# Two residual tiles turned by VectorE and two transfers instead of by TensorE, and one key weight split earlier

## The reference

```python
h = rmsnorm(x, norm_mix_w)
proj = h @ w_in                       # gated linear attention heads and differential attention heads
mixed = concatenate([o_gla, o_diff])  # both head groups, normed and gated
x = x + mixed @ w_out                 # the residual stream after the mixing branch
hc = rmsnorm(x, norm_cross_w)
q = hc @ w_cq                         # 4 heads of 256
k, v = split(rmsnorm(mem, norm_mem_w) @ w_ckv)
x = x + (softmax(q @ k.T / 16) @ v) @ w_co
return rmsnorm(x, final_norm_w)
```

## Time and profile before

| | |
|---|---|
| time, median of 3 runs | 816.72 us (815.28 to 817.65) |
| profiled execution, its own time | 814.48 us |
| its span, first to last instruction | 812.7 us |
| TensorE busy | 799.4 us, 98% |
| VectorE busy | 593.1 us, 73% |
| ScalarE busy | 422.1 us, 52% |
| mean granted TensorE clock | 0.998 of full |

### The profile page before, as it was taken

How to read it: one execution, slowest core, us unless ns; L and a number is a source line. 1 busy time by engine, 2 the same in 40 slices (tenths; PEclk the granted TensorE clock), 3 DMA queues, 4 the chain that set the end, 5 groups by cost and what they waited for, 6 DMA issues and landing times.

```text
span 812.7 us, 13040 instructions
## 1 busy us (share of the span) xinstructions
PE 799.4 (98%) x4376; PEld 669.9 (82%) x4376; DVE 593.1 (73%) x1386; ACT 422.1 (52%) x1025; POOL 98.8 (12%) x138
## 2 busy tenths in 40 slices
PE   8999999999999999999999999999999999999996
PEld 7887888888788888888888798888888888888885
DVE  6688677675678678767868877798847563367997
ACT  7766445444455345445535556543645553366453
POOL 3100111121011010111212211010010000001201
PEclk9999999999999999999999999999999999999999
DMA  8331236568365334545667368954457312107945
GB/s 283 128 84 40 85 98 170 97 111 156 66 111 112 87 95 114 108 81 98 126 132 162 108 173 269 317 125 124 146 134 177 102 66 74 57 14 153 215 86 207
DMA packets 126538, 103.41 MB, mean 127 GB/s; under 512 B 58628, under 2 KB 96648, under 8 KB 126472
## 3 DMA queue, kind: packets, MB, share of 16 engines
q1 hardware_dynamic: 98184, 66.40, 28.2%
q0 software_dynamic: 15392, 29.36, 20.1%
q10 hardware_dynamic: 12896, 6.82, 2.9%
HBM read 85.77 MB, written 33.55 MB: 147 GB/s over the span
## 4 chain that ended last, share of the span: by engine, by line
PE 83%; DVE 9%; ACT 4%; issue 2%; DMA 1%; POOL 0%; ACTq 0%; DVEq 0%
PE bank L1936 14%; PE bank L1938 14%; PE bank L1937 14%; PE banks2to L1936 9%; PE banks2to L1938 9%; PE banks2to L1937 9%; PE banks2to L2193 3%; PE banks6to L1999 3%; PE bank L2216 2%; DVE w_lo L1442 2%; DVE neg_max L1738 1%; DVE actT_lo L1441 1%; PE banks2to L2133 1%; PE bank L2218 1%; PE banks2to L2120 1%
## 5 line engine op out<-in xcount | busy, mean ns | idle before, releaser
L1938 PE MATMUL bank<-w_hi,actT_lo 128*128 128x512 f32 x412 | 161.5, 392 | 0.0
L1936 PE MATMUL bank<-w_hi,actT_hi 128*128 128x512 f32 x384 | 154.6, 403 | 0.5 <-DVE memT_lo L1441 0.2
L1937 PE MATMUL bank<-w_lo,actT_hi 128*128 128x512 f32 x384 | 149.8, 390 | 0.0
L1442 DVE SCALAR_TENSOR_TENSOR w_lo<-w_raw,vecs,w_hi 128x512 fp32r<-128x512 f32 x120 | 87.0, 748 | 24.1 <-ACT w_hi L1158 23.8
L1938 PEld LDWEIGHTS bank<-w_hi,actT_lo 128*128 128x128 f32 x412 | 77.4, 188 | 16.9
L1158 ACT ACTIVATE w_hi<-w_raw,vecs 128x512 fp32r<-128x512 f32 x120 | 83.1, 721 | 14.3 <-DMA w_raw<-in_w_ckv 8.7
L1936 PEld LDWEIGHTS bank<-w_hi,actT_hi 128*128 128x128 f32 x384 | 72.2, 188 | 16.7 <-DVE w_lo L1442 1.6
L1937 PEld LDWEIGHTS bank<-w_lo,actT_hi 128*128 128x128 f32 x384 | 72.4, 188 | 13.1
L1030 POOL TENSOR_TENSOR rs_o<-var_o,neg_half 128x1 f32<-128x1 f32 (+1 forms) x48 | 31.1, 647 | 343.8 <-DVE var_o L1766 228.5
L1938 PE MATMUL banks2to<-w_hi,actT_lo 128*128 128x512 f32 x164 | 64.0, 390 | 0.0
L1325 ACT ACTIVATE prob<-banks2to,neg_maxs 128x128 f32<-128x128 f32 (+7 forms) x64 | 46.9, 740 | 15.2 <-DVE neg_maxs L1739 15.0
(11 more groups left out here) (377 smaller groups left out, 2037.6 us busy)
## 6 DMA issues: line engine op xcount, KB each, us to landing
w_raw<-in_w_in SPq DMA_DIRECT2D x56, 256.0 KB, 3.0
out_sums<-in_w_out POOLq DMA_DIRECT2D x11, 1024.0 KB, 9.0
late_sums<-in_w_co POOLq DMA_DIRECT2D x11, 1024.0 KB, 9.2
w_raw<-in_w_ckv SPq DMA_DIRECT2D x32, 256.0 KB, 3.6
w_raw<-in_w_cq SPq DMA_DIRECT2D x32, 256.0 KB, 2.9
stage_in<-in_x SPq DMA_DIRECT2D x8, 512.0 KB, 4.6
mixT<-mixed ACTq DMA_DIRECT2D x16, 256.0 KB, 4.0
x_res<-in_x SPq DMA_DIRECT2D x8, 512.0 KB, 5.7
```

Source lines behind the costliest of these rows:

```text
L1442: return dve.scalar_tensor_tensor(dst, src, scale, hi.bitcast(F32), ALU.mult, ALU.subtract)
L1936: pe.matmul(dst, l_hi, r_hi, start=start, stop=False)
L1937: pe.matmul(dst, l_hi, r_lo, start=False, stop=False)
L1938: return pe.matmul(dst, l_lo, r_hi, start=False, stop=stop)
```

## The change

Tiles 0 and 1 of the residual take the way that tiles 4 to 7 take, with `tile_a` and `tile_b` as buffers (whole rows of 1024, so four transfers of 128 KB a tile); tiles 2 and 3 are still turned by TensorE, and their entries HT stay where they were. The entries hturn 0 and 1 stand behind xr 0 and xr 1, hback 0 and 1 at the old places of HT 0 and HT 1, and the splits HS 0 and 1 behind the HT of tiles 2 and 3. Apart from that the weight 66 is split behind K 1, ahead of the product PV 30, and no longer behind T 31.

```diff
 (stages)
             elif p == 4:
-                plan.extend([("xa", 5, t), *([("xa", 6, t)] if t < 2 else [("xr", t - 2)])])
+                plan.extend([("xa", 5, t), *([("xa", 6, t)] if t < 2 else [("xr", t - 2), ("hturn", t - 2)])])
...
-            if (p == 5 and t > 1) or (p == 6 and t < 2):
-                plan.extend([("HT", (t - 2) % 4, kk) for kk in range(2)])
+            if p == 5 and t > 1:
+                plan.extend([("hback", t - 2)])
+            if p == 6 and t < 2:
+                plan.extend([("HT", t + 2, kk) for kk in range(2)])
+                plan.extend([("HS", t, kk) for kk in range(2)])
 (with_weights)
-                where = ("Ke", 1) if k < 2 else ("T", DIFF_STEPS - 1, 1)
+                where = ("Ke", 1) if k < 3 else ("T", DIFF_STEPS - 1, 1)
 (helpers)
+        def turning_tile(t):
+            if t < 4:
+                return [(0, D, (tile_a, tile_b)[t % 2][:, :])]
+            return [(WC * j, WC, mixT[:, 6 - 2 * (t % 2) + j, 4 * P:8 * P]) for j in range(2)]
 (SyncE)
+                    for first, n, tile in turning_tile(t):
                         for band in range(P // BLK):
+                            part = tile[BLK * band:BLK * band + BLK, :]
+                            sp.dma_start(turned_rows(first, n, t, band),
...
                 elif kind == "loadw":
+                    sp.wait_ge(*turned_stored(1))
 (ScalarE)
                 elif kind == "hback":
+                    act.wait_ge(*turned_stored(t))
+                    if t < 4:
+                        act.wait_ge(*matmuls_done(("X", 4, t)))
...
                 elif kind == "HS":
+                    act.wait_ge(*residual_back(t))
 (TensorE, before a query product of the first half)
+                    if not half:
+                        pe.wait_ge(xa_dve, SPLIT_X[("HS", 1, kk)] + 1)
```

More of the change, by code:

```diff
@@ L871, in ring_job, with turned_stored, turned_no, residual_back @@
                     ps.rearrange("p (j c) -> p j c", j=4))
-        def turning_row(t):
-            return 6 - 2 * (t % 2)
-        def rest_stored():
-            return STORED * (DIFF_STEPS // 4 + 2)
+        def turning_tile(t):
+            if t < 4:
+                return [(0, D, (tile_a, tile_b)[t % 2][:, :])]
+            return [(WC * j, WC, mixT[:, 6 - 2 * (t % 2) + j, 4 * P:8 * P]) for j in range(2)]
+        def turned_stored(t):
+            first = 1 if t % 4 < 2 else 0
+            return d_mixd[t % 4], STORED * (DIFF_STEPS // 4 + (first if t < 4 else first + 2))
+        def turned_no(t):
+            return DIFF_STEPS + (t + 1 if t < 2 else t - 1)
+        def residual_back(t):
+            return d_tile[t % 4], 16 * (len(RELOADS) // 4 + (2 if t in (4, 5) else 1))
         def kept_residual(t, kk):
@@ L995, in _ @@
                     t = w[0]
-                    sp.wait_ge(md_dve, DIFF_STEPS + t - TT // 2 + 1)
-                    for j in range(2):
+                    sp.wait_ge(md_dve, turned_no(t))
+                    for first, n, tile in turning_tile(t):
                         for band in range(P // BLK):
-                            part = mixT[BLK * band:BLK * band + BLK, turning_row(t) + j, 4 * P:8 * P]
-                            sp.dma_start(turned_rows(512 * j, 512, t, band),
+                            part = tile[BLK * band:BLK * band + BLK, :]
+                            sp.dma_start(turned_rows(first, n, t, band),
                                          part.rearrange("r (b c) -> r b c", c=BLK)).then_inc(d_mixd[t % 4], 16)
@@ L1719, in _ @@
                     t = w[0]
-                    dve.wait_ge(*matmuls_done(("X", 6, 3)))
+                    if t >= 4:
+                        dve.wait_ge(*matmuls_done(("X", 6, 3)))
                     dve.wait_ge(*row_ready(t))
                     if t >= 6:
-                        dve.wait_ge(d_mixd[t % 4 - 2], rest_stored())
-                    for j in range(2):
-                        last = dve.transpose(mixT[:, turning_row(t) + j, 4 * P:8 * P], x_res[:, t, WC * j:WC * j + WC])
+                        dve.wait_ge(*turned_stored(t - 2))
+                    for first, n, tile in turning_tile(t):
+                        last = dve.transpose(tile, x_res[:, t, first:first + n])
                     last.then_inc(md_dve, 1)
@@ L1728, in _ @@
                     raw, hi, lo = kept_residual(*w)
-                    dve.wait_ge(d_tile[w[0] % 4], 16 * (len(RELOADS) // 4 + 1))
+                    dve.wait_ge(*residual_back(w[0]))
                     dve.wait_ge(xa_act, SPLIT_X[stage] + 1)
```

7 lines of the change are left out of this document (4 added, 3 removed).

## The result

The changed kernel takes 819.37 us (median of 20 runs, 817.52 to 821.82) against 815.91 for the kernel before (20 runs, 814.77 to 817.65). The ratio is 1.0044 [1.0036, 1.0052], so it is slower, by about 3.6 us. As a difference it was +0.9 us with at most +2.7; that 819.37 lies just under the forecast's upper end of 819.4 is luck, since that end was counted from a median of three runs, 816.72, and the 20 runs have 815.91. The profiled execution has a span of 818.3 us (before 812.7).

What follows compares the result with a forecast made beforehand. TensorE, busy 98% of the span, was taken as the bound. The residual part's +1.4 and the weight split's -0.5 gave +0.9 us, from a median of 816.72 to 817.6 us; range 815.0 to 819.4.

Steps and rivals of the forecast that it cites:

- Removed on TensorE: Two groups of eight transposes leave TensorE's path ahead of the first query product, 0.90 us each, 1.80 us together.
- Added on VectorE: Two 1024-wide transposes ahead of weight 112's split, 1.34 us a tile, 2.68 us; TensorE doesn't feel it.
- SyncE's queue: Four 128 KB stores take 2.2 us to issue, so load 116 is issued at 573.7 instead of 570.05.
- The landing of load 116: Weight 116, behind the stores in SyncE's queue, lands at 578.0, between bounds of 576.6 and 579.5.
- Slack: Loads of weights 116 to 119 had over 2 us to spare; the late issue alone eats that, leaving ScalarE the bound.
- ScalarE at tile 2: ScalarE comes to the copies of tile 2 at about 581.4, bounds 580.7 and 582.7.
- The chain from there: From tile 2's copies to the first query product: 4.63 + 1.05 + 3.28 + 1.2 = 10.2 us on ScalarE and VectorE.
- the query product starting with no wait: Sign of a wrong forecast; the right sign was a TensorE wait ahead of the first query product.
- Sum: First query product at 591.6 instead of 590.23, +1.4 us; with the weight split's -0.5, +0.9 us in all.
- The weight split: Splitting weight 66 ahead of PV 30 ends TensorE's wait at 479.09 for late weight 71: -0.5 us (0 to -0.85).
- Rival 4: Tile 1's stores and tile 0's reload share engines, SyncE's issues stall, 119 lands behind 582.7: 819.6 to 821 us; chance 0.11.
- Rival 2: Transfers hidden, loads land undisturbed, ScalarE meets tile 2 at 579.1; 0.9 of 1.8 us won: 815.3 us; chance 0.14.

Runs made afterwards that it cites:

- e13: Kernel before plus the eight stores of residual rows 0 and 1, without VectorE transposes or reloads, TensorE turning all four tiles: 816.36 us, ratio 1.0016.
- e6: Kernel before plus VectorE's two extra transposes into a tile nobody reads, no stores or reloads: 817.25 us, ratio 1.0023.
- e1: Kernel before with only weight 66 split ahead of PV 30: 814.93 us, ratio 0.9996.
- e5: Changed kernel without the weight split and without the eight stores of tiles 0 and 1; reloads bring stale rows: 817.21 us, ratio 1.0019.
- e15: The same kernel as e5, measured again: 816.43 us, ratio 1.0013 against the kernel before.
- e14: The same kernel as e6, measured again: 817.17 us, ratio 1.0024 against the kernel before.
- e8: Changed kernel without the weight split, tile 1's transpose and stores moved behind weights 112 and 113: 820.61 us, ratio 1.0086 against the kernel before.
- e9: e8 with tile 3's transposes behind the second last value product and six norm squares behind tile 1's splits: 823.08 us, ratio 1.0086 against the kernel before.
- e7: Changed kernel without the weight split, only tile 0 the new way, tile 1 turned by TensorE: 816.38 us, ratio 1.0007 against the kernel before.
- e10: Changed kernel without the weight split, tile 3's transposes behind the second last value product, six norm squares behind tile 1's splits: 821.05 us, ratio 1.0068.
- e4: Changed kernel without the weight split, stores of tiles 0 and 1 carrying only 256 of 1024 features: 816.28 us, ratio 1.0008 against the kernel before.
- e3: Changed kernel without the weight split, stores of tiles 0 and 1 issued on ScalarE's queue: 819.53 us, ratio 1.0045 against the kernel before.

## Why the prediction was wrong, point by point

Times behind the anchor are compared (a time of the prediction less 563.82, one of the changed kernel less 565.50).

- **Removed on TensorE**, 1.80: measured 1.80.
- **Added on VectorE**, 2.68 ahead of weight 112: measured 2.53. That weights 112 to 115 are covered: right, no wait of TensorE there.
- **SyncE's queue** was the first miss. Four stores were put at 2.2 us of issue; tile 0's took 2.58 and tile 1's 3.37, since single issues grew from 0.33 to 1.02 us as stores piled up. Load 116 was forecast at 9.88 and issued at 10.98: 1.1 late.
- **The landing of load 116 is the step that failed.** Taken was 578.0, 4.3 us after the issue, with 579.5 as upper bound; it took 5.7. Together with the queue the load landed at 16.68 where 14.18 was forecast, 2.5 late and 1.0 beyond the upper bound. The bound let the stores end at 577.0, 13.2 behind the anchor and 8.7 us after the first is issued; the last one landed at 15.6, 11.1 us after the first was issued. In e13, with the same stores and no reload, it was 9.0 us, and the load took 3.6. So what was missing is what the reload of tile 0 does to the last stores, some 2 us; the bound had it only as "a part" in the 2.5 us for the load, of which 1.1 was needed. (The 4.0 us of all engines a tile came out near the mark by luck. The 3370 packets behind that figure were not all stores; from 570.0 to 575.2, with nothing but stores under way, 4815 packets took 75.3% of the engines, 3.3 us for the 4096 of a tile. But the stores did not fill the engines either.) The rule of the Trainium skill, "DMA: Bandwidth & Descriptors", section "Queues, rings and completion order", that each transfer engine takes a queue's descriptors in ring order, pointed to the upper bound. The trace agrees: the load landed 1.1 us behind the last store of its queue.
- **Slack.** Before, 116 landed at 572.7 (570.05 and 2.7) and was split at 575.13: 2.4 us of slack. The changed kernel delays it by 2.53 on VectorE, 2.2 on SyncE and 3.0 in the transfer (5.7 for 2.7), 7.8 in all. VectorE's part alone is within 0.1 us of the slack (e6, where D grows by 1.2 through load 117), and the stores alone, 4.3 us of delay, cost 0.7 in D (e13); in the whole change all three delays reach one load. That is one reason why the parts don't add up; the other is what e13 and e6 leave out.
- **ScalarE at tile 2**: forecast 17.58, measured 585.26 - 565.50 = 19.76, 2.2 late. The upper bound was 18.9.
- **The chain from there, 10.2 us**: measured 595.37 - 585.26 = 10.1, to the end of the low parts of tile 1 (594.09 and 1.28). This part of the working was right, though it put the wait at the wrong place: TensorE waited at tile 3's transposes, 3.76 us, and then started the query product with no wait. The prediction had counted the wait at tile 3 as inside that of the query product, and had named "the query product starting with no wait" as a sign of being wrong.
- **TensorE's clock** was not priced. Behind the stall it ran at a mean of 0.57 over 4 us, and TensorE reached the query product at 595.83, 0.46 behind the chain's end. So in the changed kernel the lower clock cost at most 0.46 us; the chain would have held TensorE until 595.4 anyway.
- **Sum.** D was forecast at 27.78. With 2.18 (ScalarE), -0.1 (chain) and 0.46 (clock) it is the 30.33 measured.
- **The weight split**, -0.5: the wait at 479.09 is gone as forecast, but the time of e1 can't be told from no change. Open between 0.6 us of loss and 1.2 of gain.
- **Rivals.** Rival 4 is what happened in the main, by its mechanism (stores and reload on one set of engines, SyncE's issues growing longer), and with 819.37 it came to within 0.3 us of its range of 819.6 to 821. It had 0.11. Its condition was not met, though: load 119 landed 18.6 behind the anchor, ahead of the 18.9 that it asked for. Load 116 decided, with 3.0 us of ScalarE's work between it and the copies of tile 2. The sentence beside it, the advice of the Trainium skill, "VectorE: DVE Perf Modes", section "Rules for kernel authors", to turn 128x128 tiles on TensorE where the result may be in PSUM, the trace bears out. Rival 2 was too hopeful even in its remark that only 0.9 of the 1.8 us would be won with the transfers hidden: with no stores at all (e5, e15) nothing was won, since ScalarE came to tile 2 at 16.8 behind the anchor and not at 15.3.

What stays open: the ratios of e5, e15, e6 and e14 stand for 0.7 to 1 us more than their D explains, those of e8 and e9 for 1.5 to 2 more, and that of e7 for 1 less. Executions of one kernel spread by 3 to 4 us, in the profiles ahead of the anchor, and I did not settle whether the kernels differ there.

## What to carry to other kernels

A transfer that hides a layout change costs three things at once: the queue that issues it, the engines that carry its small packets, and every in-order engine that waits for its landing. Add the delays that reach one late transfer before comparing them with its slack, since each alone may fit and the sum not. Transfers of different queues also meet on the engines, here the stores of one tile and the reload of the tile before: ask what each one finds under way. Count as well the work that the new way moves onto the chain; 2.2 us of copies did so here, and with no store at all the saved 1.8 us were still not won. With both tiles changed, moving the waiting around (another queue, a later place, other work ahead) brought nothing; cutting the packets did, and a stall of TensorE of about 4 us has to be priced with the slower clock behind it.

## What the runs showed of the hardware

- **TensorE's clock fell after one long stall.** After idle times of 3.76 us (changed kernel) and 4.90 (e8) its mean was 0.57 over the next 4 us, after 3.99 (e10) it ran at 1.2 GHz for the next 5.4, with a matmul of 0.39 us taking 0.63. With waits of 0.69 and 1.51 us (e4) it stayed at 2.4, and with 2.51 and 1.87 (e3) it fell behind the second. In e10 this cost 2.7 us, in e3 1.7.
- **Issuing blocks the issuing engine.** A store of 128 KB in pieces of 128 bytes took SyncE 0.33 us to issue at first and up to 1.02 later in the changed kernel; in e8 a single one took 2.7, with loads and the reload still under way. On ScalarE's queue three took 3.68 us (e3), during which it split nothing.
- **A load lands about 1 us behind the last small store ahead of it in its queue, and another queue's transfer delays both.** The 256 KB load of 116 landed in 2.7 us with nothing ahead (e5), 3.4 behind four stores, with the reload issued only 1.0 us before it landed (e8), 3.6 behind eight with no reload at all (e13), 4.1 behind eight of a quarter size beside the reload (e4), 5.7 behind eight full ones beside it (changed kernel). It landed 0.9 to 1.1 us behind the last of these stores each time. In e3, with the stores on ScalarE's queue, it took 3.4.
- **Stores in pieces of 128 bytes** took 3.3 us of all 16 engines for 512 KB (4815 packets at 75.3% over 5.2 us, changed kernel).
